# A hybrid attention and MoE layer on one core: projections spread over the first head, last block by halves, logits in two tiles

## The reference

```python
h = rmsnorm(x) * (1 + scale) + shift
u = h @ w_in                                     # conv part, low-rank q, low-rank kv, rotary key
conv_out = silu(layernorm(depthwise_conv(glu(u_conv))))
k_nope, v = split(concat(cache_ckv, rmsnorm(u_kv)) @ w_ukv)   # 4 heads of 128
att = softmax((q_nope @ k_nope.T + q_rope @ k_rope.T) * c) @ v
out = concat(conv_out, att) @ w_out
x = x + gt1 * rmsnorm(out)                       # x1
h = rmsnorm(x) * (1 + sc2) + sh2                 # h2
logits = h @ [w_rg | w_re] + bias                # 4 groups, 32 experts
# best group, best two experts in it; gates from the softmaxes
y = sum(gate[e] * (silu(h @ w_gate[e]) * (h @ w_up[e])) @ w_down[e])
x = x + gt2 * rmsnorm(y)
```

## Time and profile before

| | |
|---|---|
| median of 3 runs (range) | 702.93 us (700.96 to 704.25) |
| profiled execution, its own time | 703.74 us |
| its span, first to last instruction | 701.9 us |
| busy: PE / DVE / ACT / POOL | 83% / 38% / 21% / 12% |
| DMA | 173.33 MB, mean 247 GB/s |
| mean granted TensorE clock | 0.95 |

### The profile page before, as it was taken

How to read it: one execution, slowest core, us unless ns; L and a number is a source line. 1 busy time by engine, 2 the same in 40 slices (tenths; PEclk the granted TensorE clock), 3 DMA queues, 4 the chain that set the end, 5 groups by cost and what they waited for, 6 DMA issues and landing times.

```text
span 701.9 us, 9338 instructions
## 1 busy us (share of the span) xinstructions
PE 583.8 (83%) x3734; PEld 339.9 (48%) x3734; DVE 264.5 (38%) x455; ACT 150.9 (21%) x301; POOL 81.2 (12%) x100
## 2 busy tenths in 40 slices
PE   0899999999999889989999474899899898777720
PEld 0666666555555445544455362455455454434300
DVE  2315999999743244402232460011011010100017
ACT  3320000112425344422223310101101100110125
POOL 6000002200000000001111026021121121110001
PEclk9999999999999989999999867999999999999965
DMA  9999943000007810045213951689999999999859
GB/s 339 350 393 404 405 164 140 14 0 1 1 1 276 317 74 1 1 143 217 120 61 127 420 222 26 240 348 423 421 426 423 421 424 423 423 425 424 357 212 270
DMA packets 47635, 173.33 MB, mean 247 GB/s; under 512 B 5738, under 2 KB 12235, under 8 KB 35290
## 3 DMA queue, kind: packets, MB, share of 16 engines
q1 hardware_dynamic: 39856, 158.47, 56.2%
q0 software_dynamic: 6448, 12.54, 5.6%
q10 hardware_dynamic: 1274, 1.52, 0.6%
HBM read 162.79 MB, written 17.06 MB: 256 GB/s over the span
## 4 chain that ended last, share of the span: by engine, by line
PE 61%; DMA 16%; SPq 9%; DVE 4%; ACT 3%; another core or an unknown queue 2%; issue 2%; DVEq 1%; ACTq 1%; POOLq 0%
PE ps L1365 14%; PE ps L1631 10%; PE ps L1696 8%; SPq L480 8%; DMA arena<-in_w_up 5%; PE ps L1712 5%; DMA arena<-in_w_down 5%; PE ps L1366 4%; PE ps L1429 3%; DMA arena<-in_w_ada 3%; PE ps L1383 3%; PE ps L1599 3%; PE ps L1567 3%; PE ps L1370 2%
## 5 line engine op out<-in xcount | busy, mean ns | idle before, releaser
L1696 PE MATMUL ps<-arena 128*64 128x256 f32 x992 | 112.7, 384 | 19.9 <-ACT arena L944 11.2
L1365 PE MATMUL ps<-arena 128*128 128x512 f32 x216 | 111.1, 596 | 0.7 <-issue 0.6
L1696 PEld LDWEIGHTS ps<-arena 128*64 128x64 f32 x992 | 72.8, 138 | 62.9 <-issue 12.8
L1074 DVE SCALAR_TENSOR_TENSOR arena<-arena 128x655 f32<-128x655 f32 x116 | 95.9, 906 | 0.4 <-issue 0.2
L1712 PE MATMUL ps<-arena 128*64 128x512 f32 x256 | 61.9, 627 | 18.4 <-ACT arena L944 12.9
L1370 PE MATMUL ps<-cst,arena 128*128 128x128 f32 (+2 forms) x349 | 52.8, 297 | 24.7 <-DVE arena L1013 16.1
L1631 PE MATMUL ps<-arena 128*128 128x512 f32 x160 | 69.2, 593 | 0.9 <-ACT arena L896 0.9
L1366 PEld LDWEIGHTS ps<-arena 128*128 128x128 f32 x216 | 41.0, 190 | 51.6 <-issue 51.6
L1370 PEld LDWEIGHTS ps<-cst,arena 128*128 128x128 f32 (+2 forms) x349 | 43.9, 179 | 37.3 <-issue 30.2
L1311 DVE TENSOR_TENSOR arena<-arena,ps 128x256 f32<-128x256 f32 x16 | 6.7, 421 | 116.8 <-ACT arena L950 116.8
L1326 DVE COPY arena<-ps 128x1024 f32<-128x1024 f32 x15 | 18.4, 1224 | 84.2 <-PE ps L1712 84.2
(11 more groups left out here) (269 smaller groups left out, 604.5 us busy)
## 6 DMA issues: line engine op xcount, KB each, us to landing
arena<-in_w_up SPq DMA_DIRECT2D x15, 2048.0 KB, 28.9
arena<-in_w_down SPq DMA_DIRECT2D x15, 2048.0 KB, 27.5
arena<-in_w_gate SPq DMA_DIRECT2D x14, 2048.0 KB, 27.0
arena<-in_w_ada SPq DMA_DIRECT2D x12, 2048.0 KB, 13.0
arena<-y_d SPq DMA_DIRECT2D x10, 512.0 KB, 7.2
arena<-in_w_out SPq DMA_DIRECT2D x1, 4096.0 KB, 12.6
arena<-ada_d SPq DMA_DIRECT2D x8, 512.0 KB, 8.0
x<-in_w_gate SPq DMA_DIRECT2D x2, 2048.0 KB, 25.9
```

The costliest lines, as they stand in the source:

```text
L1074: ins = dve.scalar_tensor_tensor(dst, src, w, dst, ALU.mult, ALU.add)
L1365: mm(pp(name)[:, 0:TS], lhs(k), rhs_s(k), start=k == 0, stop=k == steps - 1)
L1696: last = mm(ps[a:a + ROWS, s, n * FE:(n + 1) * FE], src[:, k, a:a + ROWS], w[:, j, k * FE:(k + 1) * FE], start=k == 0, stop=k == KD - 1)
```

## The change

- k0 and k1 stand ahead of head 0's scores, v0 to v5, k2 and k3 between its parts; ScalarE's k and v read-outs move into its loop of heads, `proj_act` goes. In every head the prompt block's scores stand ahead of the head output.
- POST: ht0 ahead of P2; rl0, rt1 and ht2 ahead of P4. P4 is computed by column halves: the first half is squared while the second is computed, the gains are multiplied in beside the squares, and 1/rms and x follow by halves. VectorE makes x times a2 beside the squares of x and then scale and shift in one instruction; GpSimd's addition goes.
- The router product goes to two column tiles (contraction halves at output rows 0 and 64), summed by the product that turns the logits back.
- The number tables are made on ScalarE; positions are read from PSUM; two steps fewer in the ids.
- Pair 0's columns are read out and multiplied by halves.

```diff
-POST = ["P0", "P1", "P2", "ht0", "P3", "rt0", "ht1", "P4", "rl0", "rt1", "ht2", "ht3", "rl1", "rt2", "rl2", "rt3",
-        "rl3", "ht4", "rt4", "rl4"]
-BETWEEN = (("rl0", "rt1", "ht2"), ("ht3", "rl1", "rt2", "rl2", "rt3", "rl3"))
+POST = ["P0", "P1", "ht0", "P2", "rt0", "ht1", "P3", "rl0", "rt1", "ht2", "P4", "rl1", "rt2", "rl2", "ht3", "rt3", "rl3",
+        "ht4", "rt4", "rl4"]
+BETWEEN = (("rl1", "rt2"), ("rl2", "ht3", "rt3", "rl3"))
...
-    names += ["state"] + [f"k{h}" for h in range(H)] + [f"v{t}" for t in range(KT)]
+    names.append("state")
...
@@ SyncE
-            landed(sp, "v5")
+            landed(sp, "k3")
...
-            sp.wait_ge(h2_last, 1)
-            sp.wait_ge(x1_ready, NT)
+            sp.wait_ge(h2_ready, NT)
@@ ScalarE
             act.dma_start(state_krope[0, 0], sto[:, KVL:]).then_inc(state_out, 16)
-            for h in range(H):
-                name = f"k{h}"
-                landed(act, name)
-                act.activation(kn[:, h, TP + PAST:], pp(name)[:, 0:TS], ACT.Copy)
-                free(act.activation(kn[:, h, 0:TP + PAST], pp(name)[:, 512:512 + TP + PAST], ACT.Copy), name)
-            for t in range(KT):
...
-            act.drain().then_inc(proj_act, 1)
             act.wait_ge(state_out, 32)
...
-                    if kind == "S":
+                    if kind == "k":
+                        landed(act, name)
+                        act.activation(kn[:, n, TP + PAST:], g[:, 0:TS], ACT.Copy)
+                        free(act.activation(kn[:, n, 0:TP + PAST], g[:, 512:512 + TP + PAST], ACT.Copy), name)
+                    elif kind == "v":
...
+                    act.activation(lg[0:G + E], pp(name)[0:G + E, 0:P], ACT.Identity, bias=rbias[:])
+                    free(act.activation(lg[DR:], pp(name)[DR:DR + G + E, 0:P], ACT.Copy), name)
...
+                if name == f"P{NT - 1}":
+                    half = h2T[1].rearrange("p k t -> p (k t)")[:, 0:512]
+                    landed(act, "rt1")
+                    act.wait_ge(p_half, 1)
+                    act.activation(half, pp(name)[:, 0:512], ACT.Square, accum_out=stat[:, 0, b:b + 1]).then_inc(pss, 1)
+                    landed(act, name)
+                    act.wait_ge(pss, NT)
+                    act.activation(half, pp(name)[:, 512:], ACT.Square, accum_out=stat[:, 3, b:b + 1]).then_inc(pss, 1)
...
+            for c, hit in enumerate(chosen):
+                act.wait_ge(oh_ready, c + 1)
+                for b in range(NT):
+                    act.activation(number[:, c, b, 0, :], hit[:, b, :], ACT.Copy, scale=cst[:, C_HI + c * NT + b:C_HI + c * NT + b + 1])
+                act.activation(number[:, c, :, 1, :], hit, ACT.Copy, scale=cst[:, C_LO:C_LO + 1]).then_inc(number_ready, 1)
...
+            act.wait_ge(t_half, 1)
+            columns_out(xT[:, 0, 0:KD // 2], ps[:, 6:7, :], D // 2).then_inc(xT_half, 1)
             act.wait_ge(e_tr, 1)
-            columns_out(xT[:, 0], ps[:, 6:8, :], D).then_inc(e_xT, 1)
+            columns_out(xT[:, 0, KD // 2:], ps[:, 7:8, :], D // 2).then_inc(e_xT, 1)
@@ VectorE
+            def second_norm(b):
...
+                dve.tensor_tensor(h2[:, b % 2, :], x[:, b, :], a2[:, v, :], ALU.mult)
...
+                dve.scalar_tensor_tensor(h2[:, b % 2, :], h2[:, b % 2, :], stat[:, 7, b:b + 1], b2[:, v, :], ALU.mult, ALU.add).then_inc(h2_ready, 1)
...
+            dve.tensor_tensor(po[:, 0:512], pp(name)[:, 0:512], gg1[:, 1, 0:512], ALU.mult)
+            dve.wait_ge(pss, NT + 1)
+            free(dve.tensor_tensor(po[:, 512:], pp(name)[:, 512:], gg1[:, 1, 512:], ALU.mult), name)
...
+            for half in (slice(0, 512), slice(512, D)):
+                dve.scalar_tensor_tensor(x[:, b, half], po[:, half], one, x[:, b, half], ALU.mult, ALU.add).then_inc(x1_ready, 1)
@@ TensorE
             for h in range(H + 1):
+                if h == 0:
+                    keys(0)
+                    keys(1)
+                    pe.wait_ge(proj_dve, 1)
                 if h < H:
+                    emptied(pe, f"k{h}")
                     scores(h, (0, 1))
...
+                else:
+                    values(0)
+                    values(1)
                 if h < H:
                     scores(h, (2, 3))
+                if h == 0:
+                    values(2)
+                    values(3)
+                if h < H:
+                    prompt_scores(h)
                 if h:
                     head_output(h - 1)
+                else:
+                    values(4)
+                    values(5)
+                    keys(2)
+                    keys(3)
                 if h < H:
-                    prompt_scores(h)
                     turned(h * NT)
...
+                    else:
+                        steps = [(k, half) for half in range(2) for k in tiles]
...
-                    for k in range(KD):
-                        last = mm(pp(name)[0:G + E, 0:P], wr[:, k, :], h2T[b % 2][:, k, :], start=k == 0, stop=k == KD - 1)
+                    for k in range(KD // 2):
+                        for at in range(2):
+                            last = mm(pp(name)[DR * at:DR * at + G + E, 0:P], wr[:, at * KD // 2 + k, :], h2T[b % 2][:, at * KD // 2 + k, :],
+                                      start=k == 0, stop=k == KD // 2 - 1)
...
+                    last = mm(pp(name)[:, 0:G + E], lg, dup[0:DR + G + E, 0:G + E], start=True, stop=True)
```

More of the change, by code:

```diff
@@ new lines, in second_norm @@
+                dve.reciprocal(stat[:, 7, b:b + 1], stat[:, 7, b:b + 1])
+                dve.drain()
+                dve.scalar_tensor_tensor(h2[:, b % 2, :], h2[:, b % 2, :], stat[:, 7, b:b + 1], b2[:, v, :], ALU.mult, ALU.add).then_inc(h2_ready, 1)
+            for b in range(NT - 1):
+                name = f"P{b}"
+                dve.wait_ge(pss, b + 1)
+                dve.tensor_scalar(stat[:, 4, b:b + 1], stat[:, 3, b:b + 1], 1.0 / D, EPS, ALU.mult, ALU.add).then_inc(pvar, 1)
+                dve.wait_ge(psd, b + 1)
+                dve.reciprocal(stat[:, 5, b:b + 1], stat[:, 5, b:b + 1])
+                dve.drain()
+                free(dve.scalar_tensor_tensor(po[:], pp(name)[:, 0:D], stat[:, 5, b:b + 1], gg1[:, min(b, 1), :], ALU.mult, ALU.mult), name)
+                dve.drain()
+                dve.tensor_tensor(x[:, b, :], x[:, b, :], po[:], ALU.add).then_inc(x1_ready, 1)
+                dve.drain()
+                second_norm(b)
@@ L1192, in _ @@
             Lg, Le = L[:, :, 0:G], L[:, :, G:]
[L1193 removed]
+            em, eq, oh1, oh2 = (wide(n) for n in range(4))
             goh, geq, pen, m1, m2, top = (narrow(5, G, 0), narrow(5, G, 1), narrow(5, G, 2), narrow(5, 1, 16), narrow(5, 1, 20), narrow(5, 1, 24))
@@ L1626, in _ @@
                             emptied(pe, f"O{h}")
-                    for k in (*range(CM, KD), *range(CM)):
+                    tiles = (*range(CM, KD), *range(CM))
+                    if b < NT - 1:
+                        steps = [(k, half) for k in tiles for half in range(2)]
+                    else:
+                        steps = [(k, half) for half in range(2) for k in tiles]
+                    for n, (k, half) in enumerate(steps):
                         if b == 0 and k == 0:
                             pe.wait_ge(mixc_ready, CM)
-                        for half in range(2):
-                            last = mm(pp(name)[:, half * 512:(half + 1) * 512], mixT[:, k, b * P:(b + 1) * P],
-                                      wo[:, k, half * 512:(half + 1) * 512], start=k == CM, stop=k == CM - 1)
+                        last = mm(pp(name)[:, half * 512:(half + 1) * 512], mixT[:, k, b * P:(b + 1) * P],
+                                  wo[:, k, half * 512:(half + 1) * 512], start=k == CM, stop=k == CM - 1)
+                        if b == NT - 1 and n == KD - 1:
+                            last.then_inc(p_half, 1)
                 elif kind == "ht":
-                    if b < NT - 1:
-                        pe.wait_ge(h2_ready, b + 1)
-                    else:
-                        pe.wait_ge(h2_last, 1)
+                    pe.wait_ge(h2_ready, b + 1)
                     for k in range(KD):
@@ L1681, in _, with rows_to_columns, gate_up @@
                 pe.wait_ge(drained[s], n)
-            def rows_to_columns(src, inc):
+            def rows_to_columns(src, inc, half_done=None):
                 for k in range(KD):
+                    if half_done is not None and k == KD // 2:
+                        last.then_inc(half_done, 1)
                     last = turn(ps[:, 6 + k // 4, (k % 4) * P:(k % 4 + 1) * P], src[:, k::KD])
                 last.then_inc(inc, 1)
-            def gate_up(s, first, src, gate, both_done):
+            def gate_up(s, first, src, gate, both_done, by_halves=False):
                 for n in range(2):
```

163 lines of the change are left out of this document (89 added, 74 removed).

## The result

The changed kernel took 707.26 us in the median of 16 runs (705.35 to 710.75), the kernel before 703.86 us in 16 runs on the same chip (700.96 to 705.72). The ratio is 1.0049 (95% interval 1.0033 to 1.0065), so it is slower by half a per cent, just at the edge of what I called no change. Ratios are of executions at the usual speed: one of e2's ten took 1018.7 us at a granted clock of 0.60 and is left out. The profiled execution has a span of 706.3 us (before 701.9) at a mean granted clock of 0.937 (before 0.95).

The account below looks back on a forecast made before the run. The end follows the start of the DMA-bound expert weight stream one for one. Terms +4.8 - 1.6 + 2.2 - 2.5 - 0.2 - 1.0 = +1.7 us, taken as +2, gave a 705.0 us median, range 699 to 711 us.

Parts of the forecast that it names:

- The first three terms of the table: Ahead of P4's end: first head +4.8 us, later heads -1.6 us, up to P4's end +2.2 us.
- The other two: P4's end to the gather's landing, -2.5 us, and the landing to load 12, -1.2 us.
- First head, +4.8: First attention head: k0's copy waits behind the state stores, then the clock is low; +4.8 us, range +4 to +7.
- Rival 1: ScalarE's queue ahead of k0: state stores cost nothing if landed before 218.7 us; whole 693.3 us; chance 0.11.
- Later heads and up to P4's end, +0.6: Later heads lose transpose waits, -1.6 us; work moved ahead of P4 and its slot wait cost +2.2 us.
- Rival 3: Router product: the two column tiles don't run side by side; whole 706.7 us; chance 0.10.
- from P4's end to the last logits, -3.5: Tail behind P4: 12.3 us instead of 15.8 us, so -3.5 us, range -2 to -5.
- The routing behind it, -0.7: Routing behind the last logits: the tables' ids come 0.7 us nearer to the logits.
- The collision: Gather issued 26.2 us behind P4 into the five weight loads, landing at 32.3 us instead of 30.6.
- rival 2: Gather beside the loads: lands at 37.5 us instead of 32.3, pair 0 at low clock; whole 711.0 us; chance 0.17.
- Pair 0, -0.2 and -1.0: Pair 0: gate starts 1.0 us earlier, low clock +0.8; unexplained stretch -1.0, between following GpSimd and TensorE.
- The stretch that I couldn't explain: Pair 0: 13.25 us of ScalarE waiting for gate and up, though TensorE's records end about 6 us sooner; taken as -1.0.

Follow-up runs that it names:

- e2: The kernel before with only the spread projections and earlier prompt scores, the state-store wait left ahead of the loop of heads; ratio 1.0048 to the kernel before.
- e1: The changed kernel with ScalarE's wait for the two state stores moved behind the loop of heads; 697.67 us, ratio 0.9912 to the kernel before.
- e4: The changed kernel with GpSimd's ten id scatters and their reload moved behind pair 0's output scatter; ratio 1.0013 to the kernel before.
- e5: The changed kernel with the ten id scatters issued two behind each of pairs 2 to 6, reload behind pair 8; ratio 1.001 to the kernel before.
- e8: The changed kernel with both the state wait behind the loop of heads (e1) and the scatters spread out (e5); 693.76 us, ratio 0.9861.
- e10: The changed kernel with three of the ten id scatters issued right behind the first two row gathers; ratio 1.0036 to the kernel before.
- e3: The changed kernel with dummy products between the router steps so TensorE does not idle in the tail; ratio 1.0041 to the kernel before.
- e7: The changed kernel with the router's logits in one column tile again; ratio 1.0078 to the kernel before.
- e9: The kernel of e3 with SyncE's load 9 held back until both row gathers have landed; ratio 1.0032 to the kernel before.
- e6: The kernel before with the same spreading of id scatters as in e5 and nothing else; 700.29 us, ratio 0.9943.
- e12: The changed kernel with e1 and e9, five id scatters during pair 0's second-round gate and up, five during pair 1's; 687.51 us, ratio 0.9771.
- e11: The changed kernel with e1, e3's warm tail, e9's held load and e10's three early scatters together; 689.87 us, ratio 0.9787 to the kernel before.

## Why the prediction was right, and where it wasn't

The forecast was 705.0 us with a range of 699 to 711 us; measured were 707.26 us. The time lies in the range, but not because the sum was right. Load 12 came 5.1 us later and not 1.7, and by the ratio the whole is 3.5 us longer and not 2; a range of 6 us on either side covers an error of that size. The first three terms of the table were right within 0.7 us. The other two were 1.4 and 2.6 us too hopeful, and the last one has the wrong sign. So the mechanism of the first three is right, and that the whole still came out as "no change" is luck: a ratio of 1.0049 where I had drawn the line at half a per cent.

**The bound** was read rightly: the end follows L12. In the nine kernels that scatter the ids within pair 0's first round it stands 243.4 to 246.1 us behind it, over 17 us of difference in L12.

**First head, +4.8, measured +4.1.** The mechanism is shown by e1: with the one wait moved, 10.5 us of the first scores' delay and the low clock behind it go, and the second head's first scores end 8.1 us sooner than before, where I had put the saving without the wait at 6.8. Rival 1 was false in its condition (the store took 9.7 us to land), but its price was about right: 11.6 us said, 9.6 us measured by the ratios and 13.3 us in the profiled spans. e2 shows that this part makes the whole loss.

**Later heads and up to P4's end, +0.6, measured +0.8.** P4's wait is 0.96 us for the 0.9 that I gave it. Rival 3 is false: the two column tiles run side by side, 1.07 us for 16 passes. The Trainium skill (TensorE: Matmul & The Clock Gate, "The mechanism") says that a weight load overlaps running matmuls only for another row group. I took this to mean that rt would keep its 1.94 us. In this trace, with both tiles on all rows, it didn't; whether the loads or only the two tiles' products overlap, the rows don't tell.

**The mis-sized step: from P4's end to the last logits, -3.5.** It measured -0.7 (15.1 us for the predicted 12.3). Every row that I used there was taken at full clock, and the change itself thinned out TensorE's work in this stretch: the granted clock fell to 0.50. It is no chance of one execution: e1, e4, e5, e8 and e10 have the same tail, and it takes 14.5 to 14.9 us there. e3 shows that this is all of it, since with the clock kept at 1.00 the stretch took 12.1 us. (My own terms for the step from ht4's start to the logits add up to 4.65 us and not to 4.8, so the sum should have read 12.15.) e7 shows it from the other side: with one tile the router's products are longer and the clock stays at 1.00. The routing behind it, -0.7, measured -0.6: from the logits to the gather's issue it was 14.5 us before and 13.9 us after.

**The collision.** The prediction had the gather run into the five loads, 32.3 us behind P4 instead of 30.6. In the changed kernel this didn't happen, because the slow tail put the gather 29.0 us behind P4, and it took 4.74 us. In e3 it did: 415.23 became 412.53 us, the transfer 7.91 us, landing 33.9 us behind P4. In e9, with the last load held, it landed 30.3 us behind P4. So a fast tail would have been given back here, as e3's was, and rival 2 (37.5 us) overstates even that case.

**Pair 0, -0.2 and -1.0, together measured +1.4.** The gate started 0.4 us sooner against the gather's landing, where I had 1.0, and its product took 9.16 us for the 7.13 us of before (+2.0 where I had +0.8), at a granted clock of 0.77. Neither reached load 12: the second round starts 20.6 us behind the gather's landing in both kernels (436.85 - 416.22 and 440.62 - 419.97), since the stretch between covers the product. The whole +1.4 is the second round's gate product, 10.04 us for the earlier trace rows's 8.69, at a granted clock of 0.70 for 0.81, a term that the sum doesn't have. The stretch that I couldn't explain follows GpSimd's scatters of ids, as e4, e5, e6 and e12 show, and not TensorE's product. GpSimd's run came 1.0 us nearer to the gather's landing, not the 2.4 us for which the prediction gives no working.

**What stays open.** The runs show that what TensorE releases well inside a run of scatters reaches ScalarE late. In the changed kernel, e3, e7, e9, e10, e11 and e12's second run the silu came 0.6 to 2.1 us behind the end of the run. In three kernels it didn't wait for the end: before, e1 and e2 it came 1.5 to 2.4 us ahead of it, still 5.7 to 6.9 us behind the product. The copy of the second round's columns came 1.9 to 3.0 us behind the run's end in all nine kernels that scatter there. With e12's early copy, this suggests that only a run's later part holds releases back. By which path it does so, no run shows. I didn't try other data or fewer rows in a scatter.

## What to carry to other kernels

When an edit moves a read-out into another loop, list every wait that now stands ahead of it on the same engine: here a wait for a small store, which the loop behind it didn't need, cost 9.6 us, and moving it made a kernel slower than its parent into one 0.9% faster. A tail with gaps has to be costed at the low clock unless something keeps TensorE busy, and a tail made faster is worth only what the next shared resource (here the loads in flight) lets through. Before work is moved into a stretch "that waits anyway", ask what that stretch costs where it lands: ten tiny scatters cost 11 to 13 us of delay beside a chain of short steps, 6.5 us inside a saturated stream, and about 1 us when five ran inside a long product ahead of the stream and five at its start.

## What the runs showed of the hardware

**Scatters of ids and releases.** While GpSimd issued indirect scatters of 128 rows of 4 bytes, one each 1.28 us, the silu behind TensorE's product came 5.7 to 8.9 us late in the seven kernels that issue all ten in one run there (before, changed, e1, e2, e3, e7, e9): in the changed kernel 438.74 us for a product recorded as over at 431.0 us. In e12 a release 1.3 us into a run came without delay. With the scatters elsewhere (e4, e5, e6, e8) it came within 0.1 us.

**Tiny writes cost DMA time.** Ten such scatters, 5 KB in all, lengthened the stream by about 6.5 us: the end stands 250.5 to 251.6 us behind L12 in e4, e5, e6 and e8, and 243.4 to 246.1 us in the others. It is not the reload of the ids, which e12 also has behind pair 8, with 245.4 us. The busy share stayed at 1.00 to 1.02, so the loss is seen in GB/s alone. The Trainium skill (DMA: Bandwidth & Descriptors, "Specifications") says that a transfer needs at least 512 bytes for the full rate and that smaller ones are read, modified and written. The trace agrees as far as it goes: busy engines at 340 GB/s where they moved 424; how the small rows are written, no run shows.
